# Six of the 192 weight slots loaded as three transfers of 112, 8 and 8 partitions

## The reference, cut to what matters

```python
def expert(acc, params):
    wgu_e, bgu_e, wd_e, bd_e, gate_e = params
    h = x @ wgu_e + bgu_e                       # w_gu: 1024 x 2048 for each of 32 experts
    hg, hu = h[:, :D_FF], h[:, D_FF:]
    hg = jnp.minimum(hg, SWIGLU_LIMIT)
    hu = jnp.clip(hu, -SWIGLU_LIMIT, SWIGLU_LIMIT)
    act = (hu + 1.0) * (hg * jax.nn.sigmoid(SWIGLU_ALPHA * hg))
    y = act @ wd_e + bd_e                       # w_down: 1024 x 1024
    return acc + gate_e[:, None] * y, None
out, _ = lax.scan(expert, acc0, (w_gu, b_gu, w_down, b_down, gates.T))
```

## Time and profile before

| | |
|---|---|
| Three runs | 1055.82, 1055.83, 1058.06 us; median 1055.83 |
| The profiled execution's own time | 1057.29 us |
| Its span in the trace | 1055.6 us |
| PE busy (matmul) | 994.2 us, 94% |
| DVE, ACT, POOL busy | 236.3, 139.2, 12.8 us |
| DMA | 421.49 MB, mean 399 GB/s |
| Granted TensorE clock | 0.99 of full speed over the span |

### The profile page before, as it was taken

One profiled execution on the slowest core, in us unless ns is written; L12 is line 12 of the kernel. 1 busy time (PEld: TensorE's weight loads), 2 busy tenths in 40 slices (PEclk: granted clock), 3 DMA queues, 4 the chain that ended last, 5 costly groups with the idle time before them and its releaser, 6 DMA issues.

```text
span 1055.6 us, 12852 instructions
## 1 busy us (share of the span) xinstructions
PE 994.2 (94%) x5756; PEld 412.0 (39%) x5757; DVE 236.3 (22%) x534; ACT 139.2 (13%) x265; POOL 12.8 (1%) x25
## 2 busy tenths in 40 slices
PE   9999989999999999999999999989999999899996
PEld 7875534433333333333333333332333333333332
DVE  3996340111111111111111111101111111110122
ACT  4134310101010101010100010100101010100103
POOL 4000000000000000000000000000000000000000
PEclk9999989999999999999999999999999999999999
DMA  9985569999999999999999999999999999999994
GB/s 322 409 365 195 184 261 392 428 418 426 428 428 427 428 426 428 426 428 427 427 428 427 426 428 427 428 430 428 426 428 427 426 428 430 427 426 427 428 427 178
DMA packets 39529, 421.49 MB, mean 399 GB/s; under 512 B 5185, under 2 KB 9329, under 8 KB 14768
## 3 DMA queue, kind: packets, MB, share of 16 engines
q1 hardware_dynamic: 37664, 420.31, 95.0%
q10 hardware_dynamic: 1808, 0.33, 0.2%
HBM read 419.56 MB, written 1.05 MB: 398 GB/s over the span
## 4 chain that ended last, share of the span: by engine, by line
PE 54%; DMA 31%; DVE 11%; ACT 2%; issue 1%; ACTq 0%; POOL 0%; DVEq 0%; POOLq 0%
PE work L1032 46%; DMA ring<-in_w_gu 31%; PE resid L1032 5%; DVE main L768 4%; DVE main L951 2%; DVE main L948 2%; DVE main L944 2%; PE work L1348 1%; ACT main L620 1%; PE work L1147 0%; PE work L1047 0%; PE work L1242 0%; DVE main L1010 0%; DVE main L775 0%; DVE ring L747 0%
## 5 line engine op out<-in xcount | busy, mean ns | idle before, releaser
L1032 PE MATMUL work<-ring,main 128*64 128x512 f32 (+1 forms) x3096 | 685.3, 593 | 26.0 <-DMA ring<-in_w_gu 22.4
L1032 PEld LDWEIGHTS work<-ring,main 128*64 128x64 f32 (+1 forms) x3096 | 223.0, 138 | 475.3 <-issue 423.3
L944 DVE TENSOR_SCALAR main<-work 128x512 f32<-128x512 f32 x32 | 22.1, 692 | 744.3 <-PE work L1032 744.3
L620 ACT ACTIVATE main<-main 128x512 f32<-128x512 f32 x32 | 20.2, 631 | 510.4 <-DVE main L944 510.4
L1032 PE MATMUL work<-ring 128*128 128x256 f32 (+2 forms) x308 | 71.9, 403 | 0.8 <-DVE ring L778 0.8
L1032 PE MATMUL resid<-main 128*128 128x512 f32 x128 | 67.6, 613 | 0.9 <-DVE main L1002 0.9
L633 ACT ACTIVATE main<-work 64x512 f32<-64x512 f32 x63 | 37.3, 592 | 222.8 <-PE work L1032 222.4
L1032 PE MATMUL work<-bgu_rows,ident 128*64 128x512 f32 x256 | 62.6, 608 | 0.0
L1032 PEld LDWEIGHTS work<-ring 128*128 128x128 f32 (+1 forms) x308 | 55.6, 186 | 16.0 <-issue 8.3
L1032 PEld LDWEIGHTS work<-select,main 128*128 128x128 bf16 x1536 | 47.3, 99 | 26.8 <-issue 26.8
L1032 PE MATMUL work<-select,main 128*128 128x64 bf16 x1536 | 51.0, 194 | 0.0
(11 more groups left out here) (178 smaller groups left out, 249.2 us busy)
## 6 DMA issues: line engine op xcount, KB each, us to landing
ring<-in_w_gu SPq DMA_DIRECT2D x128, 2048.0 KB, 39.3
ring<-in_w_down SPq DMA_DIRECT2D x62, 2048.0 KB, 39.3
ring<-in_w_in SPq DMA_DIRECT2D x3, 2048.0 KB, 14.8
ring<-in_w_in SPq DMA_DIRECT2D x4, 1024.0 KB, 12.1
ring<-in_w_out SPq DMA_DIRECT2D x2, 2048.0 KB, 19.5
ring<-in_w_down SPq DMA_DIRECT2D x3, 1024.0 KB, 43.6
main<-in_x SPq DMA_DIRECT2D x2, 512.0 KB, 4.1
result<-main SPq DMA_DIRECT2D x4, 256.0 KB, 2.7
```

Of the source, the lines that this page charges most:

```text
L620: nc.scalar.activation(sig_h, gate_h, ACT.Sigmoid, scale=SWIGLU_ALPHA).then_inc(sig_ready, 1)
L944: V.tensor_scalar(gate_h, work[:, GATE_BANK, :], SWIGLU_LIMIT, None, ALU.min).then_inc(gate_clamped, 1)
L1032: return nc.tensor.matmul(out_, lhsT, rhs, start=start, stop=stop, skip_group_check=True)
```

## The change

Of the chunks numbered 34, 62, 90, 118, 146 and 174, each is loaded by three `dma_start` instead of one: partitions 0 to 111, 112 to 119 and 120 to 127, one behind the other in the same queue. Each adds 16 to the slot's semaphore, and `uses_of` counts them, so that PE waits for all three. All other loads are as before, and the same bytes go to the same places.

```diff
+    IN_PARTS = [34 + 28 * m for m in range(6)]
+    PARTS = ((0, 112), (112, 120), (120, 128))
+
     def uses_of(e, i):
         number = NUMBER[e, i]
-        return number // SLOTS + 1
+        return sum(len(PARTS) if m in IN_PARTS else 1 for m in range(number % SLOTS, number + 1, SLOTS))
...
-            def load_chunk(e, i, s):
+            def load_chunk(number, e, i, s):
...
-                sp.dma_start(chunk(s), src).then_inc(slot_full[s], 16)
+                if number in IN_PARTS:
+                    for first, end in PARTS:
+                        sp.dma_start(chunk(s)[first:end, :], src[first:end, :]).then_inc(slot_full[s], 16)
+                else:
+                    sp.dma_start(chunk(s), src).then_inc(slot_full[s], 16)
```

More of the change, by code:

```diff
@@ L385, in _ @@
                 else:
-                    load_chunk(e, i, slot_of(e, i))
+                    load_chunk(number, e, i, slot_of(e, i))
                 if number in (CONV_SLOT, SLOTS - 1):
@@ L396, in extra @@
                 for i in range(CHUNKS):
-                    load_chunk(e, i, slot_of(E, i))
+                    load_chunk(NUMBER[E, i], e, i, slot_of(E, i))
             extras(sp, extra, experts_over(sp))
```

## The result

The changed kernel takes 1140.39 us (median of 4 runs, 1131.56 to 1142.52), the kernel before beside it 1055.82 us: ratio 1.0784, 95% interval 1.0765 to 1.0802. That is 84.6 us slower. The direction was forecast; the time lies outside the forecast range of 1053 to 1104.

What follows compares the result with a forecast made beforehand. Bound: one unpausing stream of weight loads. Each split slot takes 4.28 + 2 x 3.1 = 10.5 us instead of 4.9, +33 us over six, less the 6.7 us lead: +27, taken as +26, giving 1082 us; range 1053 to 1104.

Steps and rivals of the forecast that it cites:

- What bounds the kernel: Expert phase: one stream of loads that never pauses, 4.895 us a chunk; time lost early or late reaches the end in full.
- PE's waits begin earlier, the stream falls in six places, packets stretch beyond 0.61 us: Signs in the changed profile: GB/s falls at six places 137 us apart, rows exceed 0.61 us, PE's chunk waits begin near 400.
- The waits grow by about the loss: Sign in the changed profile: the sum of PE's waits for chunks grows by about the time lost.
- Issues and the semaphore's count at nothing: Twelve more issues on SP, hidden, 0 (4 us if the cover were gone); PE waits once for a larger number, 0.
- The narrow loads at 3.1 us each, 2 x 3.1 x 6 = 37 us: Two 8-partition loads in each of six split slots: 3.1 us each on their eight engines, between bounds of 0.61 and 4.9.
- b_down's load: Load of 32 partitions, 0.13 MB, in the old profile: 3.3 times its price, so 2.0 us for a narrow transfer.
- 112 partitions: 7 x 0.612 = 4.28 us: Wide load of each split slot: seven rows for each of 16 engines, 4.28 us instead of 4.90.
- Rival 4: Deeper stall: the 112-partition load misaligns engines and their sixteenths; 8 us a slot, +48, 1104; upper part of narrow stall's 0.68.
- The six slots cost the same: All six split slots: one cost of +5.6 us multiplied by six, +33 us before any lead.
- The lead of the early eight: From 150 to 1000 us, instruction packets make eight engines about 6.7 us later than the other, early eight.
- It pays 6.7 us first: If the narrow loads fall on the early eight, their 6.7 us lead is used first: +33 becomes +27 us.
- Balancing, the rival on the other side: Narrow rows cost 0.61 us each on the early eight, late eight gain; -2 us, 1053.8; chance 0.20.

## Why the prediction was wrong, point by point

- *What bounds the kernel*: right. One stream of loads; time lost early reaches the end in full. Slot 34 alone, loaded before 280 us when PE had a stock, still cost 7.3 us, and the last wait for a chunk moved by the whole loss.
- *PE's waits begin earlier, the stream falls in six places, packets stretch beyond 0.61 us*: right; the first wait stands at 428 us, and packets take up to 2.9 us. *The waits grow by about the loss*: only to 62.2 of 84.6 us; the rest is PE's busy time at the lower clock, which the prediction left out.
- *Issues and the semaphore's count at nothing*: right (the three column loads, ratio 1.0008).
- *The narrow loads at 3.1 us each, 2 x 3.1 x 6 = 37 us*: that narrow loads cost more than their bytes was right, and the term too large. Two loads for each of six slots add 25.0 us over the load of 112 alone, 2.1 us each; by themselves, with half rows, they gave 1.04 us, or 2.1 for a whole one. The measured row of b_down's load (2.0) was the better guide than the step up from it.
- ***112 partitions: 7 x 0.612 = 4.28 us***: this is the step that failed. I priced the wide load by the number of rows an engine gets, as if only the narrow ones changed what is written where. Measured, it takes 14.8 us, 10.6 us more than that; over six slots this is 63.3 us, and the sum of the prediction had nothing for it. In its place the runs show a stream that falls to 164 to 279 GB/s around each such load, with no narrow load near. Rival 4 named this mechanism but put it at 8 us a slot for everything together; 14.1 were needed. The halves of 64 show that it is no matter of narrowness: loads of half the partitions, neighbours all, halve the stream's rate, even with all engines booked.
- *The six slots cost the same*: taken for granted without a word, and wrong. Alone they cost 7.3, 11.3 and 15.5 us at numbers 34, 118 and 174. With the first of these for all six, the forecast would still have been 44 us and not 84.6. Nor had the prediction a term for an engine that falls behind from slot to slot; at the end one is 13 us behind the fifteen others.
- *The lead of the early eight*: it is there. In the kernel before, the later eight of the 16 rises lie 1.1 us behind the earlier eight at chunk 32 and 6.9 us at chunk 190; 6.7 was estimated. *It pays 6.7 us first*: not seen. In the changed kernel the lag doesn't shrink (0.8 us at chunk 32, 8.9 at 190), and the version meant to use the lead (the 16 small loads a slot) lost 18 us.
- *Balancing, the rival on the other side*: out. It needed 0.87 us or less a narrow load; it is 2.1, and the wide load costs by itself.

What is shown: that the loss comes from blocks of neighbouring partitions that are fewer than all (112 alone, 64 in a block against 64 alternate ones), and that it passes as slow packets on engines that are all occupied. What is argued from that: in a load of 112 neighbours, engines and pieces of the destination no longer go together for the whole load, and engines that are slow there also hold up the rows of the next chunks behind them. The DMA view supports it, with a fall of some 16 us for a slot worth 5. But the trace doesn't tell which engine or which piece of the destination a packet belongs to, and no run tried 112 partitions spread over the whole slot, which would tell the number from the block for the wide load as the alternate halves did for 64.

## What to carry to other kernels

Where a stream of loads fills the DMA engines, as here, cut a load along the free dimension or by every second partition, not into blocks of partitions: both of the first cuts were free, and 112 + 16 or 64 + 64 partitions cost some 9 to 13 us for each 2 MiB. Price each part of a split load by which partitions it takes, the large part as well as the small ones. The engines' busy share doesn't show such a loss: read GB/s beside it. And ask where the last engine stands, not only how many bytes have passed.

## What the runs showed of the hardware that I had not expected

- The DMA engines' share stays at 1.01 in windows in which they move 341 instead of 427 GB/s.
- A chunk loaded as two times 64 alternate partitions comes as fast as one of 128 (ratio 0.9999), although there are as many loads, of as many rows and with as many semaphore rises, as in the slow halves.
- In the kernel before, nothing is split, and still the 16 rises of a chunk drift apart: 2.4 us from first to last at chunk 34, 5.5 at 118, 8.5 at 174. The prediction puts this down to instruction packets; no run tests that.
- The same split slot costs 7.3 us early and 15.5 us late in the kernel; the cause is open.
- With PE idle in the stalls, its granted clock fell. The windows of the changed kernel around the last split slot:

```profile
980.00:1000.00 20.00, 19.34 (x130) 7.46 (x126) 4.30 (x9) 2.68 (x5) 0.00 (x0) 1.00 1.02 363
1000.00:1020.00 20.00, 12.17 (x34) 3.19 (x32) 0.00 (x0) 0.00 (x0) 0.00 (x0) 0.74 1.00 247
1020.00:1040.00 20.00, 16.35 (x112) 6.22 (x112) 4.30 (x9) 2.41 (x4) 0.00 (x0) 1.00 1.00 363
```

  PE is busy 12.17 of 20 us and the granted clock is 0.74 of full speed on average there, between its two levels of 1.2 and 2.4 GHz. Over the whole kernel PE was busy 22.3 us longer for it, but that time came out of waiting for loads and added nothing to the end: the last load landed when it did, and from the last wait to the last scatter it needs 1130.23 - 1087.07 = 43.16 us, as before.
